# Narrow small levels, states between the pairs, and an output projection that begins with half of its contraction

## The reference, cut to what matters

```python
# GDN, prompt tokens, per head and chunk: a unit lower triangular solve
lower = where(strict, einsum('bhntd,bhnsd->bhnts', kb, kc) * decay, 0.0)
a_mat = lower + eye(CHUNK)
sol = triangular_solve(a_mat, [v * beta | kb * exp(G)])        # u_base, w
u = u_b - w_i @ s;  o = qd_i @ s + qk_i @ u;  s = gl_i * s + kd_i^T @ u
# GLA gives o_a, GDN gives o_b; each is normed per head and gated
o_a = rmsnorm(o_a, gla_g_out) * silu(gr);  o_b = rmsnorm(o_b, gdn_g_out) * silu(dz)
o = concatenate([o_a, o_b])            # 1024 + 1024 columns
x = x + einsum('bte,ed->btd', o, w_out)   # output projection, contraction 2048
x = x + cross_attention(...);  x = x + swiglu(...)
```

## Time and profile before

| | |
|---|---|
| median of 3 runs | 1975.34 us (1969.19 to 1978.47) |
| profiled execution, its own time | 1973.66 us |
| its span | 1972.0 us |
| mean granted clock of TensorE | 0.977 of 2.4 GHz |
| TensorE busy | 1850.0 us (94%) |
| VectorE busy | 1152.9 us (58%) |
| ScalarE busy | 763.8 us (39%) |
| GpSimd busy | 244.1 us (12%) |

### The profile page before, as it was taken

The page is one execution under the profiler, slowest core; times in us unless marked ns, Lnnn a source line. Parts: engine busy times, 40 slices in busy tenths (PEclk is TensorE's granted clock), DMA queues, the critical chain, the costliest instruction groups (busy, mean ns, idle before and its releaser), DMA issues.

```text
span 1972.0 us, 34279 instructions
## 1 busy us (share of the span) xinstructions
PE 1850.0 (94%) x13811; PEld 1744.9 (88%) x13811; DVE 1152.9 (58%) x1588; ACT 763.8 (39%) x772; POOL 244.1 (12%) x226
## 2 busy tenths in 40 slices
PE   5999999858996989999999999999999999999996
PEld 3999999856886989988764999999999999999996
DVE  5888444571765647755545656666544466665443
ACT  1554544332224343334443334444333344443332
POOL 6000000000532530000000540000000000000331
PEclk9999999978998999999999999999999999999998
DMA  5555555413204556788685468888555789985452
GB/s 163 171 170 171 171 171 171 131 44 96 86 1 140 171 196 202 255 276 277 232 298 185 154 186 231 240 257 240 156 175 176 209 232 253 253 219 169 157 184 88
DMA packets 413654, 362.57 MB, mean 184 GB/s; under 512 B 11343, under 2 KB 373838, under 8 KB 412774
## 3 DMA queue, kind: packets, MB, share of 16 engines
q1 hardware_dynamic: 386198, 336.53, 55.7%
q10 hardware_dynamic: 27392, 25.17, 4.0%
HBM read 345.67 MB, written 16.19 MB: 184 GB/s over the span
## 4 chain that ended last, share of the span: by engine, by line
PE 85%; DVE 8%; ACT 3%; issue 2%; POOL 1%; DMA 0%; DVEq 0%; POOLq 0%; ACTq 0%; SPq 0%
PE ps L423 66%; PE ps L443 9%; DVE w_lo L407 2%; PE ps L1169 1%; PE ps L836 1%; ACT w_hi L400 1%; PE ps L1177 1%; PE ps L952 1%; PE ps L984 1%; PE ps L1138 1%; PE ps L1038 1%; PE ps L1029 0%; DVE cacc L536 0%; DMA raw<-in_ffn_w_up_dram 0%; DVE act_lo L1641 0%
## 5 line engine op out<-in xcount | busy, mean ns | idle before, releaser
L400 ACT ACTIVATE w_hi<-raw 128x2048 fp32r<-128x2048 f32 (+1 forms) x289 | 519.8, 1799 | 926.7 <-PE ps L423 801.5
L407 DVE TENSOR_TENSOR w_lo<-raw,w_hi 128x2048 fp32r<-128x2048 f32 (+1 forms) x289 | 629.6, 2179 | 319.5 <-ACT w_hi L400 316.3
L423 PE MATMUL ps<-act_hi,w_lo 128*128 128x264 f32 x2576 | 740.1, 287 | 12.9 <-DVE w_lo L407 9.7
L423 PE MATMUL ps<-act_lo,w_hi 128*128 128x264 f32 x2576 | 732.3, 284 | 0.0
L423 PE MATMUL ps<-act_hi,w_hi 128*128 128x264 f32 x2576 | 732.0, 284 | 0.0
L423 PEld LDWEIGHTS ps<-act_hi,w_lo 128*128 128x128 f32 x2576 | 487.6, 189 | 16.7 <-issue 8.1
L423 PEld LDWEIGHTS ps<-act_lo,w_hi 128*128 128x128 f32 x2576 | 487.9, 189 | 0.6
L423 PEld LDWEIGHTS ps<-act_hi,w_hi 128*128 128x128 f32 x2576 | 485.3, 188 | 0.0
L423 PE MATMUL ps<-ff_hi,w_lo 128*128 128x264 f32 x704 | 201.3, 286 | 4.3 <-DVE ff_lo L559 4.3
L423 PE MATMUL ps<-ff_hi,w_hi 128*128 128x264 f32 x704 | 200.8, 285 | 0.0
L423 PE MATMUL ps<-ff_lo,w_hi 128*128 128x264 f32 x704 | 200.2, 284 | 0.0
(11 more groups left out here) (369 smaller groups left out, 1936.3 us busy)
## 6 DMA issues: line engine op xcount, KB each, us to landing
raw<-in_w_in_dram SPq DMA_DIRECT2D x56, 1024.0 KB, 6.7
raw<-in_ffn_w_gate_dram SPq DMA_DIRECT2D x44, 1024.0 KB, 5.8
raw<-in_ffn_w_up_dram SPq DMA_DIRECT2D x44, 1024.0 KB, 10.4
raw<-in_ffn_w_down_dram SPq DMA_DIRECT2D x32, 768.0 KB, 4.6
raw<-in_ffn_w_down_dram SPq DMA_DIRECT2D x32, 640.0 KB, 5.8
raw<-in_w_out_dram SPq DMA_DIRECT2D x16, 1024.0 KB, 7.7
raw<-in_xa_w_q_dram SPq DMA_DIRECT2D x16, 1024.0 KB, 7.2
raw<-in_xa_w_k_dram SPq DMA_DIRECT2D x16, 1024.0 KB, 6.3
```

What stands on the lines that cost most here:

```text
L400: act.activation(w_part(ph, w_hi[b]), raw_part(ph, r, half), ACT.Copy)\
L407: dve.tensor_tensor(w_part(ph, w_lo[b]), raw_part(ph, r, half), w_part(ph, w_hi[b]), ALU.subtract)\
L423: mm = pe.matmul(ps[:, acc(ph, u), 0:ph.cols], w[b][:, k, :], v[:, kk + k, 0:ph.cols], start=first and k == 0 and m == 0, stop=last and k ...
```

## The change

- **States between the pairs.** The turns of keys and values are interleaved with the sample states of GLA; the `on_state` products of GDN stand between the pairs of the four groups instead of behind them. The GLA norm sums are halved: GpSimd adds pairs of squares first, TensorE then needs 8 instructions instead of 16. The norm factors are kept as sums until all four are there, so that Ln and Exp run once over 1056 columns each.
- **Narrow small levels.** At levels 2 to 5 the diagonal 32x32 blocks are all that matters, so the right operand of both products has 32 columns per block instead of 128 (`Tc`, `Yc`; `narrow_y`, `narrow_t`), with the left operand still 128x128 (`Ld`, `U`). VectorE updates by a predicated copy of 128x128 elements and four transposes of 32 partitions by 128 elements; at level 5 a full transpose to `Tm` follows. Products of neighbouring groups alternate. GpSimd masks once (`Ld`) instead of at every level. Levels 6 and 7 take the unmasked `Lt`, and the mask is in VectorE's predicated copies. `sample_outputs` moves behind level 7, `scale_keys` is cut in four pieces between the updates of levels 6 and 7, and so are the GLA gates, whose gains have been folded into the gate tensors earlier.
- **First halves of w_out.** Units 0 to 3 of the output projection run in two halves of eight contraction steps. The first halves (GLA outputs, `oa_hi`, `oa_lo`) need only the GLA part and run between and behind the head sums of GDN; the second halves (`ob_hi`, `ob_lo`) wait for `o_ready` 4 as all of `w_out` did. Each unit's split of weights is cut in two pieces as well (`half_split_hi`, `half_split_lo`, 128x1024 elements). Units 4 to 15 run as before.

The diff, cut to its core:

```diff
+def half_split_hi(act, u, h):
+    ph = PH["w_out"]
+    r, landed, half, b, n = unit_of(ph, 0, u)
+    k0 = 8 * (u // 2)
+    act.wait_ge(raw_landed[r], landed)
+    if h:
+        W(act, "half_done", HALF_ORDER.index(u) + 1)
+    act.activation(w_hi[b][:, k0:k0 + 8, :], raw[:, r, 8 * h:8 * h + 8, half * P:half * P + P], ACT.Copy)\
+       .then_inc(hi_split if h else N["half_hi"], 1)
...
+def half_products(pe, u, h, k_from=0, k_to=8):
+    ph = PH["w_out"]
+    b, n, k0 = (ph.u0 + u) % 2, ph.u0 + u, 8 * (u // 2)
+    hi, lo = (ob_hi, ob_lo) if h else (oa_hi, oa_lo)
+    if k_from == 0:
+        if h:
+            pe.wait_ge(lo_split, n + 1 + LO_CREDIT)
+        else:
+            W(pe, "half_lo", HALF_ORDER.index(u) + 1)
+    for k in range(k_from, k_to):
+        for m, (w, v) in enumerate(((w_lo, hi), (w_hi, lo), (w_hi, hi))):
+            mm = pe.matmul(ps[:, acc(ph, u), 0:TT], w[b][:, k0 + k, :], v[:, k, :],
+                           start=h == 0 and k == 0 and m == 0, stop=h == 1 and k == 7 and m == 2)
+    if k_to == 8:
+        mm.then_inc(units_done if h else N["half_done"], 1)
...
+    W(pool, "norm_sq", 1)
+    pool.tensor_tensor(nsq[:, 0:8:2, :], nsq[:, 0:8:2, :], nsq[:, 1:8:2, :], ALU.add).then_inc(N["gdn_qkm"], 1)
+    W(pool, "silu_g", 19)
+    for m in range(2):
+        v = gla[:, 16 + 4 * m:20 + 4 * m, :]
...
-        pool.tensor_tensor(Bt[:, 4 * g:4 * g + 4, :], Lt[:, 4 * g:4 * g + 4, :],
-                           levels[:, 1, :].unsqueeze(1).broadcast_to([P, 4, P]), ALU.mult)\
-            .then_inc(N["gdn_bt"], 1)
...
+        pool.tensor_tensor(Ld[:, 4 * g:4 * g + 4, :], Lt[:, 4 * g:4 * g + 4, :],
+                           diag[:, :].unsqueeze(1).broadcast_to([P, 4, P]), ALU.mult).then_inc(N["gdn_bt"], 1)
...
+    pairs(0)
+    pe.wait_ge(rows_copied, 1)
+    for e in range(2):
+        mm = turn(ps[:, 5, 256 + e * 32:256 + (e + 1) * 32], grow[:, e * P:(e + 1) * P])
+    mm.then_inc(N["gla_turned"], 1)
+    pe.wait_ge(columns_ready, 2)
+    pe.wait_ge(N["bst_landed"], 16)
+    on_state(0)
+    on_state(1)
+    pe.wait_ge(gla_done, 1)
+    pairs(1)
+    on_state(2)
+    norm_sum(0)
+    on_state(3)
+    norm_sum(1)
+    W(pe, "gdn_lt", 1)
+    pairs(2)
+    on_state(4)
+    norm_sum(2)
+    on_state(5)
+    norm_sum(3)
+    W(pe, "gdn_lt", 2)
+    pairs(3)
...
-            for n in range(4):
-                mm = pe.matmul(ps[:, g, n * P:(n + 1) * P], Bt[:, 4 * g + n, :], Tm[:, 4 * g + n, :],
-                               start=True, stop=True)
-            mm.then_inc(N["y_done"], 1)
...
+    def narrow_y(n):
+        g = n % 4
+        W(pe, "inv_ready", n + 1)
...
+        for i in range(4):
+            mm = pe.matmul(ps[:, Y_BANK[n % 3], i * BW:i * BW + BW], Ld[:, 4 * g + i, :], Tc[:, 4 * g + i, :],
+                           start=True, stop=True)
+        mm.then_inc(N["y_done"], 1)
+    def narrow_t(n):
+        g = n % 4
+        W(pe, "y_copied", n + 1)
...
+        for i in range(4):
+            mm = pe.matmul(ps[:, T_BANK[n % 3], i * BW:i * BW + BW], U[:, 4 * g + i, :], Yc[:, 4 * g + i, :],
+                           start=True, stop=True)
+        mm.then_inc(N["tyuy_done"], 1)
...
+    last = 4 * (SQUARE_LEVELS - 1) - 1
+    for n in range(last + 1):
+        narrow_y(n)
+        if n:
+            narrow_t(n - 1)
+        if n == 2:
+            sample_rows()
+    whole_y(SQUARE_LEVELS + 1, 0)
+    narrow_t(last)
+    whole_y(SQUARE_LEVELS + 1, 1)
+    whole_y(SQUARE_LEVELS + 1, 2)
+    both(0)
...
+    W(pe, "o_ready", 2)
+    W(pe, "gdn_ub", 1)
+    head_sums(0)
+    half_products(pe, 0, 0, 0, 4)
+    head_sums(1)
+    half_products(pe, 0, 0, 4, 8)
+    W(pe, "norm_rb", GH + 2 + 1)
+    half_products(pe, 2, 0)
+    half_products(pe, 1, 0)
+    half_products(pe, 3, 0)
     W(pe, "o_ready", 4)
-    phase_pe(pe, PH["w_out"], ow_hi, ow_lo)
+    for u in range(4):
+        half_products(pe, u, 1)
+    with pe.Fori(1, PH["w_out"].loops) as i:
+        for u in range(4):
+            out_products(pe, i, u)
...
+    for n in range(4 * (LEVELS - 2)):
+        l, g = 2 + n // 4, n % 4
+        W(act, "y_done", n + 1)
+        if l <= SQUARE_LEVELS:
+            act.activation(Yc[:, 4 * g:4 * g + 4, :],
+                           ps[:, Y_BANK[n % 3], 0:4 * BW].rearrange("p (u t) -> p u t", u=4), ACT.Copy)\
+               .then_inc(N["y_copied"], 1)
+        else:
+            act.activation(Y[:, 4 * g:4 * g + 4, :], heads_of(WHOLE_Y[g]), ACT.Copy).then_inc(N["y_copied"], 1)
...
+    gated_hi(1)
+    W(act, "gdn_sval", 1)
+    half_split_hi(act, 0, 0)
+    half_split_hi(act, 2, 0)
...
+    half_split_hi(act, 1, 0)
+    half_split_hi(act, 3, 0)
...
-    act.wait_ge(raw_landed[PH["w_out"].s0 % 2], 32 * (PH["w_out"].s0 // 2 + 1))
-    for u in range(2):
-        split(PH["w_out"], 0, u)
...
+    half_split_hi(act, 0, 1)
     for g in range(2):
         act.wait_ge(o_gated, g + 1)
-        for c in (g, 2 + g):
-            act.activation(ow_hi[:, 4 * c:4 * c + 4, :], gla[:, 16 + 4 * c:20 + 4 * c, :], ACT.Copy).then_inc(o_hi, 1)
-    run("w_out", none, "x_q")
+        act.activation(ob_hi[:, 4 * g:4 * g + 4, :], gla[:, 24 + 4 * g:28 + 4 * g, :], ACT.Copy).then_inc(o_hi, 1)
+    for u in range(1, 4):
+        half_split_hi(act, u, 1)
...
+    for n in range(4 * (LEVELS - 2)):
+        l, g = 2 + n // 4, n % 4
+        W(dve, "tyuy_done", n + 1)
...
+        if l <= SQUARE_LEVELS:
+            link(dve.copy_predicated(Tc[:, 4 * g:4 * g + 4, :],
+                                     maskc[:, l - 2, :].unsqueeze(1).broadcast_to([P, 4, BW]).bitcast(U32),
+                                     ps[:, T_BANK[n % 3], 0:4 * BW].rearrange("p (u t) -> p u t", u=4)))
+            for b in range(P // BW):
+                at = slice(BW * b, BW * b + BW)
+                ins = dve.transpose(U[at, 4 * g:4 * g + 4, at], Tc[at, 4 * g:4 * g + 4, :])
+            if l == SQUARE_LEVELS:
+                link(ins)
+                ins = dve.transpose(units(Tm, g), units(U, g))
+            ins.then_inc(N["inv_ready"], 1)
+        elif l == SQUARE_LEVELS + 1:
+            b0 = BOTH[g % 2]
+            dve.copy_predicated(tm, b3(levels[:, 0, :], 4).bitcast(U32), heads_of(b0))
+            dve.copy_predicated(um, mask, heads_of(b0 + 1)).then_inc(N["inv_ready"], 1)
+            scale_keys(g - 2) if g >= 2 else gla_gate(g)
+        else:
+            dve.copy_predicated(um, mask, heads_of(LAST_U[g])).then_inc(N["inv_ready"], 1)
+            scale_keys(g + 2) if g < 2 else gla_gate(g)
...
+    half_split_lo(dve, 0, 0)
+    half_split_lo(dve, 2, 0)
+    W(dve, "gdn_f", 6)
+    half_split_lo(dve, 1, 0)
...
+    half_split_lo(dve, 0, 1)
+    for g in range(2):
+        dve.wait_ge(o_hi, 2 + g + 1)
+        dve.tensor_tensor(ob_lo[:, 4 * g:4 * g + 4, :], gla[:, 24 + 4 * g:28 + 4 * g, :],
+                          ob_hi[:, 4 * g:4 * g + 4, :], ALU.subtract).then_inc(N["o_ready"], 1)
+    for u in range(1, 4):
+        half_split_lo(dve, u, 1)
```

More of the change, by code:

```diff
@@ L47 @@
 SQUARE_LEVELS = 5
+BW = 32
+HALF_ORDER = (0, 2, 1, 3)
+Y_BANK = (0, 2, 3)
+T_BANK = (5, 4, 6)
+WHOLE_Y = (1, 2, 3, 0)
+BOTH = (6, 4)
+LAST_U = (6, 7, 4, 5)
 UNIT_CREDIT = 2
@@ new lines, in out_products @@
+        def out_products(pe, i, u):
+            ph = PH["w_out"]
+            b, n = (ph.u0 + u) % 2, ph.u0 + 4 * i + u
+            pe.wait_ge(acc_free, ph.t0 + 4 * i + u + 1)
+            pe.wait_ge(lo_split, n + 1 + LO_CREDIT)
+            for k in range(KT):
+                hi, lo = (ob_hi, ob_lo) if k >= 8 else (oa_hi, oa_lo)
+                for m, (w, v) in enumerate(((w_lo, hi), (w_hi, lo), (w_hi, hi))):
+                    mm = pe.matmul(ps[:, acc(ph, u), 0:TT], w[b][:, k, :], v[:, k % 8, :],
+                                   start=k == 0 and m == 0, stop=k == KT - 1 and m == 2)
+            mm.then_inc(units_done, 1)
@@ new lines, in _ @@
+            whole_y(SQUARE_LEVELS + 1, 0)
[3 more added lines that the diff above has]
+            both(0)
+            whole_y(SQUARE_LEVELS + 1, 3)
+            both(1)
+            both(2)
+            whole_y(LEVELS - 1, 0)
+            both(3)
+            whole_y(LEVELS - 1, 1)
+            whole_y(LEVELS - 1, 2)
+            last_u(0)
+            whole_y(LEVELS - 1, 3)
+            for g in range(1, 4):
+                last_u(g)
@@ L1508, in _ @@
+                ins.then_inc(N["norm_rb"], 1)
+            W(act, "norm_rb", GH + 2 + 2)
             for g in range(2):
@@ L1799, in _ @@
             dve.tensor_copy(gks[:, :, :], gla[:, GH:2 * GH, T:TT]).then_inc(N["gla_qe"], 1)
+            for b in range(P // BW):
+                at = slice(BW * b, BW * b + BW)
+                dve.transpose(maskc[at, :, :], levels[at, 2:2 + 4, at])
             W(dve, "gla_mm", 1)
@@ L1950, in _ @@
[L1950 to L1957 removed]
+                W(dve, "norm_rb", GH + 2 + 2 + g + 1)
@@ new lines, in _, with out_taken @@
+            for u in range(1, 4):
+                half_split_lo(dve, u, 1)
+            dve.wait_ge(x_ready, KT)
```

(15 more changed lines are left out.)

481 lines of the change are left out of this document (267 added, 214 removed).

## The result

| | before | after |
|---|---|---|
| median of 16 runs | 1973.23 us | 1979.91 us (1974.09 to 1983.63) |
| ratio, 95% interval | | 1.0033 [1.0023, 1.0043] |
| span of the profiled execution | 1972.0 us | 1979.1 us |
| mean granted clock | 0.977 | 0.965 |

The change made the kernel slower by 6.7 us, where a gain of 26 us was forecast. The ratios leave out the few executions far above the rest of their kernel, among them the profiled one of the run with the wait filled (2834.91 us at a mean clock of 0.61), so that this run has no trace to read. I read the after trace with the stretches of the earlier trace rows, cut at the same instructions. The rows are: length, busy TensorE, weight loads, VectorE, ScalarE, GpSimd (instructions), granted clock, DMA share, GB/s.

A forecast was written before the change was run, and what follows sets the result against it. TensorE was taken as the bound, with gains only from its idle time and dropped instructions: −8.6 − 0.3 − 4.5 + 1.2 − 7.5 − 6.6 = −26.3 us against the span 1972.0, forecast 1949 us, range 1940 to 1978.

The forecast's parts named there:

- the term of levels 2 to 5: Levels 2 to 5: 32 groups at 0.89 us, sample products and a starting wait, 31.9 us, so −0.3 us.
- rival 1: Levels 2 to 5: narrow products make the clock fall to 1.2 GHz, +28 us, 1977 us; chance 0.25.
- the case that the prediction cites beside rival 1: Trainium skill's second HAM failure mode: small gaps between groups of matmuls make the clock oscillate; no size given.
- w_out: Output projection: 88.0 us, −6.6, with a 5.2 us stall before unit 4 for the third slot.
- states and pairs: First stretch: states between the pairs fill 5.75 us of idle time, fewer norm sums; 48.3 us, −8.6.
- Levels 2 to 7 together: Second and third stretches: levels 2 to 5 at 31.9 us (−0.3), levels 6 and 7 at 19.9 us (−4.5).
- Final products: Stretch before the tail: same matmuls, 16.30 us, but a late ScalarE copy for F4 adds 1.2 us.
- Tail: Before the second halves: head sums and first halves keep TensorE busy, 15.5 us against 23.02, −7.5.
- the first case of rival 4: Before unit 4: fourth slot's load shares the queue with the third, up to 5.5 us more, 1954; in the forecast's 0.57.
- Rivals 2 and 3: Levels 2 to 5: VectorE bounds them, +19, 1968 us, chance 0.10; or narrow matmuls cost half, 1941 us, chance 0.05.

The follow-up runs named there:

- the run with the wait filled: Changed kernel, still 32 columns, with ten extra 128-column matmuls where TensorE waited 2.16 us behind the first Y of level 2: 1979.62 us, ratio 1.0032.
- the run with 128 columns: Changed kernel with each product of levels 2 to 5 streaming 128 columns, the 32 read four times over: 1952.76 us, ratio 0.9898.
- the run without halves: 128 columns in levels 2 to 5 of the changed kernel, with the first and second halves of w_out undone: 1958.83 us, ratio 0.9924.

## Why the prediction was wrong

**The step that failed** is the term of levels 2 to 5, and with it the chance of rival 1. The sum took 0.89 us a group, by the rows of 8 and 128 columns; that is right for the engine at full clock (0.89 in the run with 128 columns). It then gave the clock falling a chance of 0.25, because it had "kept 1.00 through all of levels 2 to 5" and because the products with the states lie in a stretch of 0.95. Both rows speak of stretches in which nearly all instructions stream 128 or 256 columns, whatever their left operand; neither says anything of narrow streaming, and the narrow ones of the earlier trace rows stood where the clock was low already (0.50 from 397.0 to 398.5 us). The runs show that it is the streamed width: 32 columns lose the clock with and without the wait and in either kernel, 128 keep it. A group of eight then took 1.71 us and the levels 55.68 us where the sum had 31.9. The Trainium skill, TensorE: Matmul & The Clock Gate, What's actually happening, has the clock set by how busy TensorE has been; here it is busy for 58.17 of 58.17 us at 0.50, so busy time as the profile counts it isn't what decides. Nor is it the case that the prediction cites beside rival 1, which is one of gaps: these 58.17 us have none. How narrow streaming brings the fall about stays open.

**Rival 1** was right in mechanism and nearly in size: +28 against a kernel at full clock, 1977 us; measured 1979.9 − 1952.8 = 27.1 us, of which 24.3 in levels 2 to 5 (55.68 − 31.39) and 2.2 in levels 6 and 7, whose first 6.6 us still ran at half clock. The measured 1979.91 lies 2 us above the range; the largest of the other misses is w_out with 3.4 us, and states and pairs follow with 1.3.

**The other terms**, read from the run with 128 columns (span 1950.7, where the sum said 1945.7). States and pairs: 48.3 forecast, 49.6 measured, both counted from behind the key-query sum; the idle time went completely (49.99 of 49.99 us busy), but 1.3 us less of the busy time did than I took off. Levels 2 to 7 together: 51.8 forecast, 53.2 measured; the waits were there where I put them (2.08 us for Yc, 2.0 us for the last update), and one of 0.6 us for the full transposes of level 5 that I didn't have. Final products 17.4 (17.5), with the wait of 0.84 us for the copies behind the half splits. Tail 15.3 (15.5): TensorE's own work closed it, as said. The size was right, and the reason only in part: the run without halves shows that 5.9 of the 7.7 us come without them and with the two splits still in place, by the gain products, which I had named, and by the low parts of the GLA outputs, which the sum left out without saying so.

**w_out** was mis-sized, 91.0 against 88.0. The stall stands where it was forecast and for the reason given, but it is 7.3 us and not 5.2: the third slot is in 14.7 us after the start of the second halves (637.79 − 623.09), where the sum had 12.5. It lands 14.9 us after the issue of the memory rows, 12.8 before; the fourth slot is issued 3.4 us behind it now, 16 us before. That fits the first case of rival 4, which I priced at up to 5.5 more, and it was 2.1; no run moves the fourth slot alone. The 12 units behind the stall took 71.9 us, 0.9 more than the 69.6 + 1.4 that I gave them with a low clock at the start.

**Rivals 2 and 3** did not come: VectorE had 0.2 us to spare per group, and narrow products at full clock cost what wide ones do.

## What to carry to other kernels

A float32 matmul that loads a left operand of 128x128 for itself alone was not made shorter by a narrow right operand here (1.97 against 2.05 us for 16 instructions), and a run of such matmuls halved TensorE's clock with no idle time in the trace. So look at the granted clock of the stretch, not at busy shares, and where a block structure shrinks the moving side, try padding it back and leave the smaller copies to the other engines. When work is moved forward to fill a tail, follow each queue behind the point where it ended before: the load that four units of work hid is exposed where the work of two is left, and the order of two transfers on one queue was then worth 6 us.

## What the runs showed of the hardware

- TensorE ran at 1.2 GHz for 58 us while the profile has it busy without a gap. In the first 51.6 us of them 32 columns were streamed for each load of 128x128 (small sample products apart), in the last 6.6 us 128 in all but one group.
- Between 32 and 128 columns there are mixed cases: 64 columns stayed at 0.50 behind a wait of 2.1 us, and without it seven executions of ten took the long time, the one with a trace among them; 96 fell with the wait and came back after 13.7 us, and without the wait didn't fall. What the chip looks at to decide is not something that these runs tell.
- The same 2 MB slot landed 8.4 us after its issue when it went ahead of the memory rows, and 13.6 us behind them.
